# The first loads of a two-block transformer kernel in quarters and halves, with 11 warm-up matmuls in place of 16

## Chip, cores and metric

One core of one Trainium2 chip. The metric is device time of one execution in microseconds (us), lower is better.

## What is computed

Two blocks in sequence on a stream of 256 tokens with 1,024 features, all in float32. The part that the change touches is the very first projection of the first block, in which index queries for sparse attention are made from the input:

```python
q, k, v, g, qi, wi, ki = jnp.split(x @ w_in, cuts, axis=-1)
q = apply_rope(q.reshape(b, s, N_HEADS, HEAD_DIM), cos, sin)
...
qi = apply_rope(qi.reshape(b, s, IDX_HEADS, IDX_DIM), cos, sin)
ki = apply_rope(ki[:, :, None, :], cos, sin)[:, :, 0, :]
```

Some 150 such weight chunks follow: the rest of the attention, a second mixer, memory cross-attention, convolution and feed-forward layers.

## The kernel before

All weights are streamed from HBM in chunks of 1 MB (128 partitions x 2 halves x 1,024 columns) through four slots of `raw`. SP issues every load of the stream (lines 419 to 456). The first four chunks are issued at once, between them the input (`x_half`, line 425, into `h`, the residual stream, 8 tiles of 128 features), the indexer's small weights (`kiw`, kept in `v`), the constants `cs` and the vectors `vec`. Every later chunk waits until its slot has been split.

A product in float32 is done as three passes of a rounded format. ScalarE copies a half chunk into `wh`, which rounds it (`hi`, line 1079, copy at 1090). VectorE subtracts that from `raw` and keeps the rest in `wl` (`lo`, line 1592, at 1598). The input is split in the same way into `xh` and `xl`, two tiles at a time (`x_high`, line 1141; `x_low`, which executes at line 1668). TensorE multiplies high by high, high by low and low by high.

TensorE starts with `WARM_UP` matmuls on ones (line 816), whose results are not used. Then `project_tokens` (line 574) does the index queries, chunk by chunk: a half chunk has 12 products of 512 columns (2 token tiles x 2 feature tiles x 3 passes, line 594). For chunks 0 and 1 it goes in the order high x high, high x low of the input, low x high of the weights, so that the roundings can arrive late; chunk 0 needs four input tiles, two for each half, and chunk 1 the other four. Among the products of chunk 1 stand 16 small key products (`indexer_keys`, line 821, two passes each), eight behind each half. Chunks 2 to 5 are the queries (`qa`). Their code has the evacuations and rotations of earlier chunks woven in by tables of hooks and calls:

```python
hi(0)
act.wait_ge(x_in[0], 16)
x_high(0, None)
x_high(1, None)
hi(1)
...
chunks("qi", units(0))
chunks("qa", units(2), between={(1, 0): keep_indexer, (1, 1): memory_in, (2, 0): lambda: relu(0),
```

The order on each engine is the order of the program. ScalarE, after the rounding of half-chunk 6 (the first half of chunk 3), copies the two finished index-query banks out of PSUM (`rope_raw`, line 1125), then rounds half-chunk 7. VectorE makes the rest of half-chunk 7 and then rotates the first copy (`rotate`, line 1632, executing at lines 1626 and 1646). TensorE turns the rotated heads with four transposes (`turn_unit`, line 826, at 834); the first turn is hooked in after the first token tile of chunk 2's second half, the second after that of chunk 3's first half. Roundings beyond the first two chunks also wait for `w_used`, which counts the half chunks that TensorE has finished with.

Of the kernel before, what the change touches and what calls it, by code (L numbers as in the profile page):

```python
# [60 lines left out]
NCST = _at  # L61


WARM_UP = 16


class Phase:
# [132 lines left out]
def build(nc, w, xt, memt, vecs, cst, wkw, dft, rpb, gain, out):  # L200
    ctx = ExitStack()
    with ctx:
# [3 lines left out]
        def sem(name):  # L206
            return ctx.enter_context(nc.semaphore(name))
# [154 lines left out]


        raw_full = [sem(f"raw_full{i}") for i in range(RAW_SLOTS)]
        first_half = sem("first_half")
        x_in = [sem(f"x_in{i}") for i in range(2)]
        const_in, kiw_in = sem("const_in"), sem("kiw_in")
        mem_in, m_saved, m_back = sem("mem_in"), sem("m_saved"), sem("m_back")
        k_saved, k_back = sem("k_saved"), sem("k_back")
# [50 lines left out]
        def _(sp):  # L420
# [1 line left out]
                sp.dma_start(raw[:, slot, :, :], w[n]).then_inc(raw_full[slot], 16)  # L422


            def x_half(i):
                sp.dma_start(h[:, 4 * i:4 * i + 4, :], xt[:, 4 * i:4 * i + 4, :]).then_inc(x_in[i], 16)

            sp.dma_start(raw[:, 0, 0, :], w[0][:, 0, :]).then_inc(first_half, 16)
            x_half(0)
            sp.dma_start(raw[:, 0, 1, :], w[0][:, 1, :]).then_inc(raw_full[0], 16)  # L430
            x_half(1)
            load(1, 1)
            sp.dma_start(kiw, wkw).then_inc(kiw_in, 16)
            load(2, 2)
            sp.dma_start(cs[:, :], cst).then_inc(const_in, 16)
# [24 lines left out]
        def _(pe):  # L460
# [113 lines left out]
            def project_tokens(name, oh, ol, ready=None, hooks={}, tile0=0, order=(0, 1, 2)):  # L574
# [4 lines left out]
                for c in range(p.n):  # L579
                    n = p.n0 + c  # L580
                    slot = n % 2
                    for half in range(2):
                        early = ready is not None and c < 2
                        if early:

                            hi_, lo_ = ready(4 * c + 2 * half)
                            pe.wait_ge(*hi_)
                            pe.wait_ge(hi_ready, 2 * n + half + 1)
                        else:
                            pe.wait_ge(lo_ready, 2 * n + half + 1)  # L590

# [12 lines left out]
                            if c >= 2 and c % 2 == 0 and half == 0:  # L604
                                pe.wait_ge(evac[p.reader], p.base + c - 1 + t)

                        if early:
                            for q in order:
                                if q == 1:
                                    pe.wait_ge(lo_ready, 2 * n + half + 1)  # L610
                                if q == 2:
                                    pe.wait_ge(*lo_)
                                for t in range(2):
                                    for e in range(2):
                                        product(t, e, q, q == order[-1])
# [460 lines left out]
        def _(act):  # L1076
            chain = Chain(act, chain_act)

            def hi(h_):

                if h_ >= 2 * NCHUNK:
                    return
                n, j = divmod(h_, 2)
                if h_ == 0:
                    act.wait_ge(first_half, 16)
                elif j == 0 or h_ == 1:
                    act.wait_ge(raw_full[n % RAW_SLOTS], 16 * (n // RAW_SLOTS + 1))
                if h_ >= 4:
                    act.wait_ge(w_used, h_ - 3)
                act.activation(wh[:, n % 2, j, :], raw[:, n % RAW_SLOTS, j, :], ACT.Copy).then_inc(hi_ready, 1)  # L1090
# [140 lines left out]
            def units(u0):  # L1231
                return lambda c, t, b: rope_raw(u0 + 2 * c + t, t, b)

            hi(0)
            act.wait_ge(x_in[0], 16)
            x_high(0, None)
            x_high(1, None)
            hi(1)
            act.wait_ge(x_in[1], 16)
            x_high(2, None)  # L1240
            x_high(3, None)
            hi(2)
# [339 lines left out]
        def _(dve):  # L1582
# [9 lines left out]
            def lo(h_):  # L1592

                if h_ >= 2 * NCHUNK:
                    return
                n, j = divmod(h_, 2)
                dve.wait_ge(hi_ready, h_ + 1)
                dve.tensor_tensor(wl[:, n % 2, j, :], raw[:, n % RAW_SLOTS, j, :],  # L1598
                                  wh[:, n % 2, j, :].bitcast(F32), ALU.subtract).then_inc(lo_ready, 1)

# [165 lines left out]
            def plain_low(name, tiles, first):  # L1766
# [8 lines left out]
                                          ALU.subtract).then_inc(dve_evac, 1)  # L1775
                return f

            lo(0)
            x_low(0, "first", None)
            x_low(1, "first", None)  # L1780
            lo(1)
            x_low(2, "first", None)
# [594 lines left out]
```

## Time and profile before

| | |
|---|---|
| median of 3 runs | 991.11 us (990.96 to 991.43) |
| span of the profiled execution | 989.2 us |
| that span against the median | 1.9 us less |
| TensorE matmul busy | 972.1 us (98%) |
| VectorE, ScalarE, GpSimd busy | 69%, 56%, 21% |
| weights moved by SP's queue | 160.66 MB of 172.93 |
| mean granted TensorE clock | 0.998 |

The profile gives no total time of its own for the profiled execution, only its span from first to last instruction; times inside it count from the start of the span. A row names engine, line, tiles and duration; a bracket tells how long the engine stood idle before and what ended that. PEld is TensorE's weight load, which can run ahead of the matmul before it; SPq is SP issuing a transfer.

### The profile page before, as it was taken

How to read it: one execution, taken by the hardware profiler on the slowest of the kernel's cores; microseconds unless marked ns; L12 is line 12 of the kernel's file. 1: busy time of each engine (PE TensorE's matmuls, PEld its weight loads, DVE VectorE, ACT ScalarE, POOL GpSimd, SP SyncE). 2: the span in 40 equal slices, each digit the busy share in tenths (PEclk: the TensorE clock that was granted, in tenths of full speed). 3: DMA queues.
4: the chain of work that ended last, by engine and by line, in shares of the span. 5: the costliest groups of instructions: out<-in, count | busy, mean ns of one | idle time of the engine just before them, and what ended most of it. 6: DMA issues, size and time to landing. Idle time of an engine off the chain costs nothing.

```text
span 989.2 us, 16695 instructions
## 1 busy us (share of the span) xinstructions
PE 972.1 (98%) x6532; PEld 879.3 (89%) x6532; DVE 686.6 (69%) x1056; ACT 556.1 (56%) x856; POOL 209.3 (21%) x199
## 2 busy tenths in 40 slices
PE   9999989999999999999999999999999999999997
PEld 8779759989988988798899899999898989989985
DVE  5789785854666687665556779776687665767973
ACT  5556673665765474555355466555445555546662
POOL 0002034300344440012003005221044301202610
PEclk9999999999999999999999999999999999999999
DMA  9634425465334447246414655457546432555441
GB/s 363 241 132 166 175 87 208 162 221 214 128 128 141 174 133 271 108 171 213 150 64 170 213 186 187 181 194 281 186 170 255 163 135 93 198 183 181 172 152 43
DMA packets 24831, 172.93 MB, mean 175 GB/s; under 512 B 2752, under 2 KB 2880, under 8 KB 4416
## 3 DMA queue, kind: packets, MB, share of 16 engines
q1 hardware_dynamic: 23040, 160.66, 45.6%
q10 hardware_dynamic: 1728, 11.40, 3.0%
q8 instruction: 42, 0.69, 0.3%
q14 instruction: 21, 0.17, 0.1%
HBM read 166.81 MB, written 5.24 MB: 174 GB/s over the span
## 4 chain that ended last, share of the span: by engine, by line
PE 93%; DVE 2%; ACT 2%; DMA 1%; issue 1%; POOL 0%; SPq 0%; ACTq 0%; DVEq 0%
PE banks L506 38%; PE banks L594 16%; PE banks L512 14%; PE banks L514 7%; PE banks L504 6%; PE banks L656 4%; PE banks L710 1%; DMA raw<-w 1%; PE banks L761 1%; PE banks L762 1%; DVE work L1725 1%; PE banks L743 1%; PE banks L917 1%; PE banks L834 0%; DVE work L1737 0%
## 5 line engine op out<-in xcount | busy, mean ns | idle before, releaser
L1598 DVE TENSOR_TENSOR wl<-raw,wh 128x1024 fp32r<-128x1024 f32 x300 | 379.7, 1275 | 157.4 <-ACT wh L1090 156.0
L1090 ACT ACTIVATE wh<-raw 128x1024 fp32r<-128x1024 f32 x300 | 313.2, 1054 | 180.6 <-PE banks L506 76.1
L512 PE MATMUL banks<-xx,wh 128*128 128x512 f32 x544 | 192.5, 398 | 0.0
L506 PE MATMUL banks<-xx,wh 128*128 128x256 f32 x1024 | 190.3, 284 | 0.0
L506 PE MATMUL banks<-yy,wh 128*128 128x256 f32 x1024 | 187.8, 285 | 0.1
L506 PEld LDWEIGHTS banks<-xx,wh 128*128 128x128 f32 x1024 | 161.4, 192 | 1.4 <-issue 0.5
L506 PEld LDWEIGHTS banks<-yy,wh 128*128 128x128 f32 x1024 | 160.4, 192 | 0.7 <-issue 0.5
L514 PE MATMUL banks<-xx,wl 128*128 128x256 f32 x544 | 151.8, 279 | 0.0
L506 PE MATMUL banks<-xx,wl 128*128 128x256 f32 x512 | 144.8, 283 | 0.0
L506 PE MATMUL banks<-yy,wl 128*128 128x256 f32 x512 | 138.6, 283 | 0.0
L512 PEld LDWEIGHTS banks<-xx,wh 128*128 128x128 f32 x544 | 102.0, 187 | 22.7
L594 PE MATMUL banks<-wh,xx 128*128 128x512 f32 x352 | 113.2, 400 | 1.6 <-ACT kt L1258 0.7
L514 PEld LDWEIGHTS banks<-xx,wl 128*128 128x128 f32 x544 | 102.6, 189 | 0.3
L506 PEld LDWEIGHTS banks<-yy,wl 128*128 128x128 f32 x512 | 98.2, 192 | 0.2
L506 PEld LDWEIGHTS banks<-xx,wl 128*128 128x128 f32 x512 | 98.1, 192 | 0.1
L594 PEld LDWEIGHTS banks<-wh,xx 128*128 128x128 f32 x352 | 65.6, 188 | 18.0 <-issue 3.1
L594 PE MATMUL banks<-wl,xx 128*128 128x512 f32 x176 | 64.9, 391 | 0.0
L2185 POOL TENSOR_TENSOR work<-work,qz 128x512 f32<-128x512 f32 x18 | 29.2, 1624 | 134.3 <-ACT work L1513 133.0
L2148 POOL TENSOR_TENSOR acc<-work 128x256 f32<-128x256 f32 x9 | 9.2, 1027 | 201.0 <-ACT work L1139 201.0
L1147 ACT ACTIVATE xx<-h,vec 128x256 fp32r<-128x256 f32 x48 | 21.8, 502 | 43.9 <-DVE h L1709 32.7
L2151 POOL TENSOR_TENSOR acc<-acc,work 128x256 f32<-128x256 f32 x27 | 29.8, 1102 | 71.5 <-ACT work L1139 70.5
L1952 DVE TENSOR_TENSOR qz<-banks,qz 128x512 f32<-128x512 f32 x30 | 20.7, 690 | 29.4 <-ACT qz L1107 25.0
(221 smaller groups left out, 1449.3 us busy)
## 6 DMA issues: line engine op xcount, KB each, us to landing
raw<-w SPq DMA_DIRECT2D x149, 1024.0 KB, 4.8
m_scratch<-yy ACTq DMA_DIRECT2D x2, 1024.0 KB, 5.9
k_scratch<-kt ACTq DMA_DIRECT2D x2, 1024.0 KB, 8.2
kt<-k_scratch ACTq DMA_DIRECT2D x2, 1024.0 KB, 5.8
yy<-m_scratch ACTq DMA_DIRECT2D x2, 1024.0 KB, 6.0
raw<-w SPq DMA_DIRECT2D x2, 512.0 KB, 5.2
h<-xt SPq DMA_DIRECT2D x2, 512.0 KB, 6.1
v<-memt ACTq DMA_DIRECT2D x1, 1024.0 KB, 7.7
```

What stands on the lines that cost most here:

```text
L504: return pe.matmul(b[:, j, at], weights, o_[:, kk, :], start=k0 + k == 0 and q == 0, stop=k0 + k == KT * p.deep - 1 and q == 2, skip_group ...
L506: return pe.matmul(b[:, j, :], weights, o_[:, kk, :], start=k0 + k == 0 and q == 0 and (j == 0 or not both_open), stop=k0 + k == KT * p.de ...
L512: pe.matmul(b[:, j, :], wh[:, slot, j, k * P:k * P + P], operand[:, :, tile0 + k0 + k, :], start=k0 + k == 0, stop=False, skip_group_check ...
L514: return pe.matmul(b[:, j, 0:S], wl[:, slot, j, k * P:k * P + P], oh[:, tile0 + k0 + k, :], start=False, stop=k0 + k == KT * p.deep - 1, s ...
L594: mm = pe.matmul(bank[p.pair + t][:, :], (oh, oh, ol)[q][:, tile0 + k, t * P:t * P + P], (wh, wl, wh)[q][:, slot, half, e * 2 * CW:(e + 1) ...
L656: mm = pe.matmul(bank[(p.pair ^ 2 * block) + t][:, :], (yh, yh, yl)[q][:, k, t * P:t * P + P], (wh, wl, wh)[q][:, slot, half, e * 2 * CW:( ...
L1090: act.activation(wh[:, n % 2, j, :], raw[:, n % RAW_SLOTS, j, :], ACT.Copy).then_inc(hi_ready, 1)
L1147: ins = act.activation(xh[:, m, :], h[:, m, :], ACT.Copy, scale=vc(gain, m))
L1598: dve.tensor_tensor(wl[:, n % 2, j, :], raw[:, n % RAW_SLOTS, j, :], wh[:, n % 2, j, :].bitcast(F32), ALU.subtract).then_inc(lo_ready, 1)
L1952: chain(dve.tensor_tensor(d, b[0], d, ALU.add))
L2151: chain(pool.tensor_tensor(acc[:, :], acc[:, :], part[:, 0, :], ALU.add))
L2185: pool.tensor_tensor(wk3(7 + c % 2), a, b, ALU.mult).then_inc(pf_ready, 1)
```

## The change

The first half of chunk 0 and the first half of the input are each loaded in two quarters, in turn: weights, input, weights, input. The second half of the input stays one transfer. Chunk 1 is loaded in two halves, each with a semaphore of its own. The roundings, the rests and the products of the first half chunk follow by quarters. The warm-up is 11 matmuls.

```diff
-WARM_UP = 16
+WARM_UP = 11
...
-            sp.dma_start(raw[:, 0, 0, :], w[0][:, 0, :]).then_inc(first_half, 16)
-            x_half(0)
+            def x_tiles(i, a, b):
+                sp.dma_start(h[:, a:b, :], xt[:, a:b, :]).then_inc(x_in[i], 16)
+
+            Q = HALF // 2
+            sp.dma_start(raw[:, 0, 0, 0:Q], w[0][:, 0, 0:Q]).then_inc(first_quarter, 16)
+            x_tiles(0, 0, 2)
+            sp.dma_start(raw[:, 0, 0, Q:], w[0][:, 0, Q:]).then_inc(first_half, 16)
+            x_tiles(1, 2, 4)
             sp.dma_start(raw[:, 0, 1, :], w[0][:, 1, :]).then_inc(raw_full[0], 16)
-            x_half(1)
-            load(1, 1)
+            x_tiles(2, 4, 8)
+            sp.dma_start(raw[:, 1, 0, :], w[1][:, 0, :]).then_inc(second_half, 16)
+            sp.dma_start(raw[:, 1, 1, :], w[1][:, 1, :]).then_inc(raw_full[1], 16)
...
+                        if first:
+                            for e in range(2):
+                                pe.wait_ge(hi_ready if e else hi_first, 1)
+                                for t in range(2):
+                                    product(t, e, 0, False)
+                                if e == 0:
+                                    pe.wait_ge(*lo_)
+                                for t in range(2):
+                                    product(t, e, 2, False)
+                            for e in range(2):
+                                pe.wait_ge(lo_ready if e else lo_first, 1)
+                                for t in range(2):
+                                    product(t, e, 1, True)
...
-            hi(0)
+            act.wait_ge(first_quarter, 16)
+            act.activation(wh[:, 0, 0, 0:HALF // 2], raw[:, 0, 0, 0:HALF // 2], ACT.Copy).then_inc(hi_first, 1)
             act.wait_ge(x_in[0], 16)
             x_high(0, None)
+            hi(0)
+            act.wait_ge(x_in[1], 16)
             x_high(1, None)
             hi(1)
-            act.wait_ge(x_in[1], 16)
+            act.wait_ge(x_in[2], 16)
...
+            dve.wait_ge(hi_first, 1)
+            dve.tensor_tensor(wl[:, 0, 0, 0:HALF // 2], raw[:, 0, 0, 0:HALF // 2],
+                              wh[:, 0, 0, 0:HALF // 2].bitcast(F32), ALU.subtract).then_inc(lo_first, 1)
+            x_low(0, "first", None)
             lo(0)
-            x_low(0, "first", None)
```

SP's queue from the start of the program, before (`w` is the stream, `xt` the input):

```order
L428 DMA raw<-w 128x1024
L426 DMA h<-xt 128x1024
L430 DMA raw<-w 128x1024
L426 DMA h<-xt 128x1024
L422 DMA raw<-w 128x2048
L433 DMA v<-wkw 128x576
L422 DMA raw<-w 128x2048
L435 DMA cs<-cst 128x1664
L436 DMA vec<-vecs 128x240
L422 DMA raw<-w 128x2048
```

and after the change:

```order
L430 DMA raw<-w 128x512
L427 DMA h<-xt 128x512
L432 DMA raw<-w 128x512
L427 DMA h<-xt 128x512
L434 DMA raw<-w 128x1024
L427 DMA h<-xt 128x1024
L436 DMA raw<-w 128x1024
L437 DMA raw<-w 128x1024
L438 DMA v<-wkw 128x576
L423 DMA raw<-w 128x2048
L440 DMA cs<-cst 128x1664
L441 DMA vec<-vecs 128x240
```

Three transfers are added ahead of the indexer's weights; bytes and their order by chunk are the same, and chunk 3 still comes last.

ScalarE from its first rounding to the first half of chunk 3, before:

```order
L1090 ACTIVATE wh<-raw 128x1024 [waits first_half]
L1144 ACTIVATE xx<-h 128x512 [waits x_in0]
L1144 ACTIVATE xx<-h 128x512
L1090 ACTIVATE wh<-raw 128x1024 [waits raw_full0]
L1144 ACTIVATE xx<-h 128x512 [waits x_in1]
L1144 ACTIVATE xx<-h 128x512
L1090 ACTIVATE wh<-raw 128x1024 [waits raw_full1]
L1090 ACTIVATE wh<-raw 128x1024
L1090 ACTIVATE wh<-raw 128x1024 [waits w_used,raw_full2]
L1090 ACTIVATE wh<-raw 128x1024 [waits w_used]
L1090 ACTIVATE wh<-raw 128x1024 [waits w_used,raw_full3]
```

and after the change:

```order
L1259 ACTIVATE wh<-raw 128x512 [waits first_quarter]
L1168 ACTIVATE xx<-h 128x512 [waits x_in0]
L1106 ACTIVATE wh<-raw 128x512 [waits first_half]
L1168 ACTIVATE xx<-h 128x512 [waits x_in1]
L1114 ACTIVATE wh<-raw 128x1024 [waits raw_full0]
L1168 ACTIVATE xx<-h 128x512 [waits x_in2]
L1168 ACTIVATE xx<-h 128x512
L1114 ACTIVATE wh<-raw 128x1024 [waits second_half]
L1114 ACTIVATE wh<-raw 128x1024 [waits raw_full1]
L1114 ACTIVATE wh<-raw 128x1024 [waits w_used,raw_full2]
L1114 ACTIVATE wh<-raw 128x1024 [waits w_used]
L1114 ACTIVATE wh<-raw 128x1024 [waits w_used,raw_full3]
```

The first rounding is cut in two with an input rounding between, and the first half of chunk 1 waits for a transfer of its own; from chunk 2 on the row of ScalarE is as it was.

TensorE's first half chunk, before and then after:

```order
L594 MATMUL banks<-wh,xx 128x512 [waits hi_ready,x_hi]
L594 MATMUL banks<-wh,xx 128x512 x3
L594 MATMUL banks<-wh,xx 128x512 [waits x_lo]
L594 MATMUL banks<-wh,xx 128x512 x3
L594 MATMUL banks<-wl,xx 128x512 [waits lo_ready]
L594 MATMUL banks<-wl,xx 128x512 x3
```

```order
L601 MATMUL banks<-wh,xx 128x512 [waits hi_first,x_hi]
L601 MATMUL banks<-wh,xx 128x512
L601 MATMUL banks<-wh,xx 128x512 [waits x_lo]
L601 MATMUL banks<-wh,xx 128x512
L601 MATMUL banks<-wh,xx 128x512 [waits hi_ready]
L601 MATMUL banks<-wh,xx 128x512 x3
L601 MATMUL banks<-wl,xx 128x512 [waits lo_first]
L601 MATMUL banks<-wl,xx 128x512
L601 MATMUL banks<-wl,xx 128x512 [waits lo_ready]
L601 MATMUL banks<-wl,xx 128x512
```

The same 12 products, with four waits by quarter in place of three by half.

## Rows read from the trace of the kernel before

**Rows 1.** Page, parts 1 and 4: busy time, and the chain that ended last.

```profile
PE 972.1 (98%) x6532; PEld 879.3 (89%) x6532; DVE 686.6 (69%) x1056; ACT 556.1 (56%) x856; POOL 209.3 (21%) x199
...
PE 93%; DVE 2%; ACT 2%; DMA 1%; issue 1%; POOL 0%; SPq 0%; ACTq 0%; DVEq 0%
```

**Rows 2.** Timeline of SP, first 6 us: start, duration, issue.

```profile
0.75 0.39 SPq L428 DMA_DIRECT2D raw<-w  x1
...
3.38 0.50 SPq L433 DMA_DIRECT2D v<-wkw  x1
...
5.41 0.46 SPq L422 DMA_DIRECT2D raw<-w  x1
```

**Rows 3.** Timeline of ScalarE, 0 to 27 us.

```profile
4.78 1.06 ACT L1090 ACTIVATE wh<-raw 128x1024 fp32r<-128x1024 f32 x1 [2.75 <-DMA raw<-w]
6.02 1.15 ACT L1144 ACTIVATE xx<-h 128x512 fp32r<-128x512 f32 x2 [0.18 <-DMA h<-xt]
8.15 1.06 ACT L1090 ACTIVATE wh<-raw 128x1024 fp32r<-128x1024 f32 x1 [0.98 <-DMA raw<-w]
9.46 1.15 ACT L1144 ACTIVATE xx<-h 128x512 fp32r<-128x512 f32 x2 [0.25 <-DMA h<-xt]
11.93 2.01 ACT L1090 ACTIVATE wh<-raw 128x1024 fp32r<-128x1024 f32 x2 [1.31 <-DMA raw<-w]
...
20.04 1.06 ACT L1090 ACTIVATE wh<-raw 128x1024 fp32r<-128x1024 f32 x1 [2.89 <-DMA raw<-w]
21.01 1.07 ACT L1125 ACTIVATE work<-banks 128x512 f32<-128x512 f32 x2
21.96 1.06 ACT L1090 ACTIVATE wh<-raw 128x1024 fp32r<-128x1024 f32 x1
25.34 1.06 ACT L1090 ACTIVATE wh<-raw 128x1024 fp32r<-128x1024 f32 x1 [2.32 <-PE banks L594]
```

**Rows 4.** Timeline of TensorE's matmuls, 0 to 14 us (x32: two passes each).

```profile
1.00 5.67 PE L816 MATMUL banks<-ones 128*128 128x128 f32 x32 [1.00 <-POOL half L2141]
6.70 2.24 PE L594 MATMUL banks<-wh,xx 128*128 128x512 f32 x8
...
9.69 1.98 PE L594 MATMUL banks<-wh,xx 128*128 128x512 f32 x8
11.51 1.07 PE L594 MATMUL banks<-wl,xx 128*128 128x512 f32 x4
13.13 2.08 PE L594 MATMUL banks<-wh,xx 128*128 128x512 f32 x8 [0.56 <-ACT wh L1090]
```

**Rows 5.** Timeline of VectorE, 22.5 to 31 us.

```profile
23.05 1.23 DVE L1598 TENSOR_TENSOR wl<-raw,wh 128x1024 fp32r<-128x1024 f32 x1 [0.70 <-ACT wh L1090]
24.20 1.29 DVE L1626 TENSOR_TENSOR work<-work,cs 128x512 f32<-128x512 f32 x2
25.52 0.76 DVE L1646 TENSOR_TENSOR work<-work 128x256 f32<-128x256 f32 x2
26.43 1.23 DVE L1598 TENSOR_TENSOR wl<-raw,wh 128x1024 fp32r<-128x1024 f32 x1 [0.16 <-ACT wh L1090]
```

**Rows 6.** Timeline of TensorE's weight loads: the first two turns.

```profile
26.33 0.47 PEld L834 LDWEIGHTS banks<-cs,work 128*128 128x128 f32 x4 [0.15 <-DVE work L1646]
...
29.71 0.42 PEld L834 LDWEIGHTS banks<-cs,work 128*128 128x128 f32 x4 [0.33 <-DVE work L1646]
```

**Rows 7.** Two stretches: length, busy per engine (instructions), granted clock, DMA share, GB/s.

```profile
5.50:7.00 1.50, 1.47 (x12) 1.28 (x11) 1.13 (x1) 1.32 (x3) 0.00 (x0) 1.00 0.84 249
7.00:12.00 5.00, 5.00 (x23) 3.90 (x22) 3.73 (x6) 2.46 (x5) 0.00 (x0) 1.00 1.03 426
```

**Rows 8.** Timeline of TensorE: warm-up passes around 4.5 and around 5.4 us.

```profile
4.15 0.85 PE L816 MATMUL banks<-ones 128*128 128x128 f32 x3
...
5.06 0.61 PE L816 MATMUL banks<-ones 128*128 128x128 f32 x4
```

**Rows 9.** DMA issues of the first 10 us: KB each, us from issue to landing.

```profile
v<-wkw SPq DMA_DIRECT2D x1, 288.0 KB, 9.3
```

More of the change, by code:

```diff
@@ L364, in build @@
         raw_full = [sem(f"raw_full{i}") for i in range(RAW_SLOTS)]
-        first_half = sem("first_half")
-        x_in = [sem(f"x_in{i}") for i in range(2)]
+        first_quarter, first_half, second_half = sem("first_quarter"), sem("first_half"), sem("second_half")
+        hi_first, lo_first = sem("hi_first"), sem("lo_first")
+        x_in = [sem(f"x_in{i}") for i in range(3)]
         const_in, kiw_in = sem("const_in"), sem("kiw_in")
@@ L422, in load @@
                 sp.dma_start(raw[:, slot, :, :], w[n]).then_inc(raw_full[slot], 16)
-            def x_half(i):
-                sp.dma_start(h[:, 4 * i:4 * i + 4, :], xt[:, 4 * i:4 * i + 4, :]).then_inc(x_in[i], 16)
-            sp.dma_start(raw[:, 0, 0, :], w[0][:, 0, :]).then_inc(first_half, 16)
-            x_half(0)
+            def x_tiles(i, a, b):
[5 more added lines that the diff above has]
+            x_tiles(1, 2, 4)
             sp.dma_start(raw[:, 0, 1, :], w[0][:, 1, :]).then_inc(raw_full[0], 16)
-            x_half(1)
-            load(1, 1)
+            x_tiles(2, 4, 8)
+            sp.dma_start(raw[:, 1, 0, :], w[1][:, 0, :]).then_inc(second_half, 16)
+            sp.dma_start(raw[:, 1, 1, :], w[1][:, 1, :]).then_inc(raw_full[1], 16)
             sp.dma_start(kiw, wkw).then_inc(kiw_in, 16)
@@ L583, in project_tokens @@
                         early = ready is not None and c < 2
+                        first = n == half == 0
                         if early:
@@ L587, in project_tokens @@
                             pe.wait_ge(*hi_)
-                            pe.wait_ge(hi_ready, 2 * n + half + 1)
+                            if not first:
+                                pe.wait_ge(hi_ready, 2 * n + half + 1)
                         else:
@@ L605, in free @@
                                 pe.wait_ge(evac[p.reader], p.base + c - 1 + t)
-                        if early:
+                        if first:
[11 more added lines that the diff above has]
+                                    product(t, e, 1, True)
+                        elif early:
                             for q in order:
@@ L1085, in hi @@
                     act.wait_ge(first_half, 16)
-                elif j == 0 or h_ == 1:
+                    act.activation(wh[:, 0, 0, HALF // 2:], raw[:, 0, 0, HALF // 2:], ACT.Copy).then_inc(hi_ready, 1)
+                    return
+                elif h_ == 2:
+                    act.wait_ge(second_half, 16)
+                elif j == 0 or h_ in (1, 3):
                     act.wait_ge(raw_full[n % RAW_SLOTS], 16 * (n // RAW_SLOTS + 1))
@@ L1597, in lo @@
                 dve.wait_ge(hi_ready, h_ + 1)
+                if h_ == 0:
+                    dve.tensor_tensor(wl[:, 0, 0, HALF // 2:], raw[:, 0, 0, HALF // 2:],
+                                      wh[:, 0, 0, HALF // 2:].bitcast(F32), ALU.subtract).then_inc(lo_ready, 1)
+                    return
                 dve.tensor_tensor(wl[:, n % 2, j, :], raw[:, n % RAW_SLOTS, j, :],
```

## Prediction

> **What bounds the kernel now.** I read the page first: TensorE is busy for 972.1 of 989.2 us, and 93% of the chain that ended last runs through it [rows 1]. So an earlier start counts only if no later wait of TensorE takes it back. The change touches the first 12 us, so next come the timelines of that stretch: SP for when transfers are issued, ScalarE for when they land, TensorE for what it does meanwhile.
>
> All first transfers sit in SP's queue by 5.9 us [rows 2]. ScalarE works them off in order, and each start behind a DMA wait marks a landing [rows 3]: first half of chunk 0 at 4.78, first half of x at 6.02, second half of chunk 0 at 8.15, rest of x at 9.46, chunk 1 at 11.93, chunk 3 at 20.04. TensorE warms up from 1.00 to 6.67, starts the 24 products of chunk 0 at 6.70, has issued them by about 12.4, and starts chunk 1 at 13.13, just after its rounding (11.93 + 1.06 = 12.99) [rows 3, 4]. This wait of about 0.7 us is the only long one near the front; the page and the critical chain end it with the landing of chunk 1.
>
> The place that decides comes 13 us later and is easily missed. The first turn of rotated heads (line 834) lies inside chunk 2's products. TensorE's weight load for it stood idle 0.15 us at 26.33 until VectorE had ended the rotation [rows 6]; the matmul before it hid that wait, so it cost nothing. Follow it back. The rotation ends at 25.52 + 0.76 = 26.28 and sits directly behind the rounding rest of 23.05 [rows 5]; that one follows ScalarE's rounding of 21.96; ahead of this stand two copies from 21.01 and the rounding from 20.04, with no idle time between them; and that one waited 2.89 us for chunk 3 to land [rows 3]. So from 20.04 to 26.33 there is a second chain, **landing of chunk 3, ScalarE, VectorE, turn**, which TensorE's own progress does not move, and in the kernel before TensorE reaches its end at the same moment as that chain does. Slack: none, within 0.15 us.
>
> **The change, part by part.**
>
> *Warm-up, 16 to 11.* Each warm-up is two passes. The last ones ran at 0.61 us for four overlapped (about 0.11 us a pass), the ones at 4.15 took 0.85 us for three (about 0.21 us a pass) [rows 8], which I read as the change from the 1.2 to the 2.4 GHz level (the granted clock behind it is 1.00 [rows 7]). Five fewer take off 10 x 0.11 = 1.1 us: the warm-up ends near 5.6 instead of 6.67. Work ahead of that is the same, so I expect the level to rise at the same time, shortly before 5 us.
>
> *Quarters.* The first quarter of weights and of x need 256 KB each. Together they are as many bytes as landed at 4.78 before, so the first product can start after that landing and one rounding of x of about 0.6 us (half of the 1.15 us pair [rows 3]): near 5.5, not 6.70. ScalarE's roundings are the same columns in more instructions; the added fixed part lies in DMA waits. The second half of chunk 0 does not arrive sooner, as no byte ahead of it is gone: 8.15, rounded at 9.21, first product near 9.35. Its 12 products, at 0.2275 us each (eight from 9.69 to 11.51 [rows 4]), end their issue near 12.1. TensorE's time won in the first half is lost waiting here.
>
> *Chunk 1 in halves.* Its first half needs 512 KB behind x: 9.46 + (11.93 - 9.46)/2 = 10.7, rounded by 11.76, product at 11.9. TensorE is there at 12.1. So chunk 1 starts at about 12.1 instead of 13.13: **1.05 us gained at that point**.
>
> *Where it goes.* Chunk 1, chunk 2's first half and the key products run without a wait, so TensorE reaches the first turn 1.05 us sooner, near 25.3. There it waits for the second chain, which starts with chunk 3. The order ahead of chunk 3 holds the same bytes, and the queue is full, so the landing keeps its place. The gain is given back at the turn, all of it. What remains is small: ScalarE's rounding at 25.34 waited 2.32 us for TensorE [rows 3], and through it VectorE stood idle 0.16 us at 26.43 [rows 5]. That wait goes, and the second turn, where the weight load waited 0.33 us and the matmul issue lost some of it [rows 6], can come up to 0.15 us sooner. I take -0.1 us.
>
> *What the smaller pieces cost the stream.* SP issues three more transfers, at about 0.45 us each [rows 2]: chunk 3 is issued near 7 instead of 5.41, still 13 us ahead of its landing, so nothing. But one megabyte now moves in 2 KB rows instead of 4 KB ones, and chunk 1 in 4 KB rows. The trace has no 2 KB row. The nearest is the 288 KB of indexer weights in 2.3 KB rows: landed at 3.38 + 9.3 = 12.68 [rows 2, 9], 0.77 us behind chunk 1, or 383 GB/s, where chunk 1's megabyte took 2.47 us, 424 GB/s. At that rate a megabyte costs 2.74 us: +0.27 us on everything behind it. Lower bound: nothing or a gain, since the start of the stream is not at full rate anyway (from 5.5 to 7.0 us it moved 249 GB/s, after that 426 [rows 7], 0.6 us lost); upper bound +0.6 us, if the small rows meet as long a slow stretch again. I take +0.27, the price of the nearest row. Size alone did not slow a queued transfer: the first half of x took 6.02 - 4.78 = 1.24 us for 512 KB, 423 GB/s, as fast per byte as chunk 1. The Trainium skill ("DMA: Bandwidth & Descriptors", section Measured) says the opposite, that transfers should be batched to a megabyte or more; its table has 138 GB/s at 64 KB and 341 at 1 MB, so by it, as an estimate, the first megabyte in quarters would lose 0.6 us or more against the rows' 2.47. Its figures are for transfers issued by GpSimd; these rows, queued from SP, disagree.
>
> **Sum.** +1.05 us gained at chunk 1 and given back at the turn = 0; -0.1 behind the turn; +0.27 for chunk 3's later landing: +0.17 us. The profiled span of 989.2 us lies 1.9 us under the median of 991.11, which is time around the span that the change leaves alone. 991.11 + 0.17 = **991.3 us**, own range 990.8 to 991.9. That 16 warm-ups end later than the first landing, or that the first quarter may land hardly sooner than the half did because most of its time is not bytes, changes nothing here: the slack in front of the second half of chunk 0 takes it up (that half starts at 9.35; the first is through near 8.4, which is 5.5 plus 12 products and two short waits).
>
> **Rivals.**
>
> *The front gain stays.* If chunk 3 lands sooner too, the turn moves with it. For it: the slow stretch from 5.5 to 7.0 us falls on the second half of chunk 0 (8.15 - 6.02 = 2.13 us for 512 KB, against 1.24 for x); with another cut it may go, which is worth 0.6 us to all that follows. Against it: no byte is saved, and most of 20 us of landing time runs at 420 GB/s. Price: from -0.6 to the full -1.05 us, 990.1 us.
>
> *The halves of chunk 1 run slowly too.* The half of chunk 0 above took 0.89 us more than a half of x of the same size and shape. If that comes from reading half rows of the weights, chunk 1's two halves each pay it: +1.8 us on chunk 3, at the turn +1.6, 992.7 us. Against it: a slow stretch that belongs to the start of the program would look the same.
>
> *Slower: the clock does not rise in time.* With 11 warm-ups the steady stretch ends 1.1 us sooner, and then come gaps (x's rest, the second half's wait near 8.4 to 9.3). In the trace the level rose under steady passes from 1.00 on, and the next work came at once [rows 4, 8]. If it has not risen before the gaps, products cost nearly twice as much: 0.2275 x 0.21/0.11 = 0.43 us. All 24 would then take 24 x 0.2 = 4.8 us longer; warm-ups end near 6.2, chunk 0 near 16.5, chunk 1 starts 3.3 us later than now, and this side of the turn has no slack: 994.2 us. It decides from about five products at the low level on (1.05 us / 0.2); fewer are absorbed. Against it: nothing before 5 us changes, where the rise lay. The Trainium skill ("TensorE: Matmul & The Clock Gate", Part 1) says that the throttle is released by activity and that the moment varies from run to run; the pace in this trace agrees on the first, and one profile cannot show the second.
>
> **Chances.** Forecast 0.66, front gain stays 0.18, slow halves 0.10, clock 0.06. The range from 989.9 to 992.3 holds the first two with the spread of the runs (0.5 us) and part of the third. A measurement of this kernel tells about 0.2%, 2 us, from no change. Faster by more than that needs nearly twice the front gain: 0.04. Slower by more: the clock case and the worst of the slow halves: 0.08. Within: 0.88.
>
> **What would show it.** Right: warm-up over near 5.6, first product near 5.5, a gap before the second half's products near 9.3, chunk 1's products from about 12.1, and then **a new idle time of about 1 us of TensorE near 25.3 to 26.5, ahead of the first turn, ended by VectorE's rotation**, with ScalarE's rounding of chunk 3 still starting near 20.0 to 20.6. Wrong: no such wait, or chunk 3's rounding before 19.6 (the gain stays) or after 21 (slow halves); passes of 0.43 us in chunk 0 (the clock).

## The result and the profile after

| | before | change |
|---|---|---|
| median, measured together (9 runs each) | 991.19 us (990.96 to 991.49) | 993.41 us (992.51 to 994.56) |
| ratio | | 1.0024, 95% interval 1.0015 to 1.0032 |
| profiled execution: time, span | span 989.2 us | 992.51 us, span 990.7 us |
| mean granted TensorE clock of the profile | 0.998 | 0.998 |

The change is slower by 2.2 us, where 0.2 were forecast. The profiled execution is the fastest of its nine, 1.5 us longer in span than that of before; so the profile explains 1.5 of the 2.2 us, and the spread of the runs, 2 us wide where before it was half of one, is a question of its own.

ScalarE's timeline after the change. A line is start, duration, engine, source line, operation, tiles; the bracket gives the idle time before and what ended it.

```profile
4.12 0.63 ACT L1259 ACTIVATE wh<-raw 128x512 fp32r<-128x512 f32 x1 [2.08 <-DMA raw<-w]
...
7.96 0.64 ACT L1168 ACTIVATE xx<-h 128x512 fp32r<-128x512 f32 x1 [1.95 <-DMA h<-xt]
9.81 1.06 ACT L1114 ACTIVATE wh<-raw 128x1024 fp32r<-128x1024 f32 x1 [1.22 <-DMA raw<-w]
11.11 1.16 ACT L1168 ACTIVATE xx<-h 128x512 fp32r<-128x512 f32 x2 [0.24 <-DMA h<-xt]
12.40 1.07 ACT L1114 ACTIVATE wh<-raw 128x1024 fp32r<-128x1024 f32 x1
13.66 1.06 ACT L1114 ACTIVATE wh<-raw 128x1024 fp32r<-128x1024 f32 x1 [0.20 <-DMA raw<-w]
...
21.79 1.06 ACT L1114 ACTIVATE wh<-raw 128x1024 fp32r<-128x1024 f32 x1 [2.87 <-DMA raw<-w]
...
25.94 1.07 ACT L1114 ACTIVATE wh<-raw 128x1024 fp32r<-128x1024 f32 x1 [1.17 <-PE banks L601]
```

The first quarter of the weights is there at 4.12, but the second quarter of the input only at 7.96, and the second half of chunk 0 at 9.81, where before it landed at 8.15 [rows 3]: **1.66 us late**. From there on hardly anything more is lost: chunk 3 comes at 21.79 against 20.04, 1.75 us late.

TensorE's matmuls, same stretch and columns:

```profile
1.00 5.07 PE L836 MATMUL banks<-ones 128*128 128x128 f32 x22 [1.00 <-POOL half L2175]
5.72 2.45 PE L601 MATMUL banks<-wh,xx 128*128 128x512 f32 x8
8.01 1.08 PE L601 MATMUL banks<-wl,xx 128*128 128x512 f32 x4
11.01 2.08 PE L601 MATMUL banks<-wh,xx 128*128 128x512 f32 x8 [1.93 <-ACT wh L1114]
12.93 1.08 PE L601 MATMUL banks<-wl,xx 128*128 128x512 f32 x4
13.85 1.98 PE L601 MATMUL banks<-wh,xx 128*128 128x512 f32 x8
...
28.08 0.66 PE L854 MATMUL banks<-cs,work 128*128 128x128 f32 x4 [0.88 <-DVE work L1677]
```

The products start 0.98 us sooner (5.72 against 6.70 [rows 4]) and then stop for 1.93 us in front of the second half of chunk 0. Chunk 1 starts at 13.85, 0.72 us later than before (13.13). And at the first turn TensorE waits once more, 0.88 us, for VectorE's rotation. VectorE and the weight loads of the two turns, first VectorE:

```profile
25.94 1.28 DVE L1657 TENSOR_TENSOR work<-work,cs 128x512 f32<-128x512 f32 x2
27.26 0.76 DVE L1677 TENSOR_TENSOR work<-work 128x256 f32<-128x256 f32 x2
```

```profile
28.07 0.42 PEld L854 LDWEIGHTS banks<-cs,work 128*128 128x128 f32 x4 [1.30 <-DVE work L1677]
...
31.21 0.47 PEld L854 LDWEIGHTS banks<-cs,work 128*128 128x128 f32 x4 [0.15 <-DVE work L1677]
```

The first turn stands at 28.07 instead of 26.33 [rows 6], 1.74 us later, as much as chunk 3 is late. Up to the second turn 0.24 us come back (31.21 - 28.07 = 3.14, before 29.71 - 26.33 = 3.38), and 1.74 - 0.24 = 1.5 us is the difference of the spans.

Where the stream lost it: stretches of the change's core, with length, busy time of PE, PEld, DVE, ACT, POOL, granted clock, DMA share and, last, GB/s; then the same stretch of before.

```profile
2.00:8.50 6.50, 6.50 (x31) 6.01 (x30) 1.95 (x3) 2.45 (x5) 0.00 (x0) 1.00 0.83 261
...
8.50:16.00 7.50, 5.58 (x25) 4.31 (x24) 5.57 (x6) 4.43 (x6) 0.00 (x0) 1.00 1.02 422
```

```profile
2.00:8.50 6.50, 6.47 (x37) 5.81 (x36) 2.43 (x3) 2.59 (x5) 0.00 (x0) 1.00 0.92 325
```

From 2.0 to 8.5 us the change moves 261 GB/s against 325, that is 64 GB/s x 6.5 us = 0.42 MB less, or 1.0 us at the full rate of 422; from 8.5 on it runs as fast as before. The rest of the 1.66 us is not in this view, but in another record of the trace: each transfer raises its semaphore in 16 steps, read here as one for each of the 16 DMA engines, and a landing is the last of them. For the second half of chunk 0 the steps lie between 7.07 and 8.13 us in before, with a mean of 7.57, and between 7.36 and 9.79 in the change, with a mean of 8.54. So the mean is 0.97 us late, which fits the bytes, and the last step another 0.69: the engines have drifted apart. For chunk 3 they are still 2.47 us apart (19.29 to 21.76), in before 1.06 (18.96 to 20.02).

### The profile page after: what moved, and what is told of

It reads as the page before. It is cut to its first block, busy times and chain, and to the rows that moved or that the text cites. A ratio compares the mean times of both kernels' runs of the same rounds, so it can differ in the third digit from the quotient of the medians.

```text
span 990.7 us, 16680 instructions
## 1 busy us (share of the span) xinstructions
PE 971.3 (98%) x6522; PEld 878.3 (89%) x6522; DVE 687.2 (69%) x1057; ACT 556.8 (56%) x857; POOL 209.3 (21%) x199
## 4 chain that ended last, share of the span: by engine, by line
PE 92%; DVE 2%; ACT 2%; DMA 1%; issue 1%; SPq 1%; POOL 0%; ACTq 0%; DVEq 0%
PE banks L511 37%; PE banks L601 15%; PE banks L517 14%; PE banks L519 7%; PE banks L509 6%; PE banks L676 4%; DMA raw<-w 1%; PE banks L730 1%; PE banks L781 1%; PE banks L782 1%; PE banks L763 1%; DVE work L1756 1%; PE banks L937 1%; PE banks L854 0%; DVE work L1768 0%
```

## The experiments

Two theories stood after this reading. **Stream**: the 2 KB rows of the quarters hold up the first 8 us, and the rest follows from that. **Clock**: the shorter warm-up and the gap behind the quarters cost TensorE its level. The experiments first took the change apart. The landings (starts of ScalarE's roundings, one profile each) of the kernels that are compared most are these:

| kernel | 2nd half of chunk 0 | chunk 1, all of it | chunk 3 | median, us |
|---|---|---|---|---|
| before | 8.15 | 11.93 | 20.04 | 991.19 |
| weight_quarters | 8.51 | 12.25 | 20.36 | 991.51 |
| input_quarters | 8.83 | 12.58 | 20.68 | 991.62 |
| not_in_turn | 9.20 | 12.97 | 21.09 | 992.6 |
| quarters_only | 9.58 | 13.33 | 21.46 | 993.32 |
| the change | 9.81 | 13.66 | 21.79 | 993.41 |
| late_rows | 8.49 | 12.55 | 20.61 | 991.59 |
| halves_only | 8.21 | 12.05 | 21.47 | 992.29 |
| halves_order | 8.16 | 12.01 | 17.73 | 990.28 |
| warm11_only | 8.29 | 12.08 | 20.20 | 991.26 |
| before_order | 8.40 | 12.20 | 17.92 | 991.15 |

In the first six rows the distance from the second half of chunk 0 to chunk 3 is 11.85 to 11.98 us: whatever is lost is lost ahead of that half. How much a landing varies by itself shows where nothing ahead of it was changed: in before, halves_only, halves_order and its repetition, warm11_only and before_order the second half of chunk 0 comes between 8.15 and 8.40.

### The parts of the change

**warm16**: the change with the old warm-up.

```diff
-WARM_UP = 11
+WARM_UP = 16
```

> The change with 16 warm-up matmuls. Theory stream (the smaller first transfers delay the stream, and chunk 3's late landing sets the first turn): the same as the change, 993.4 us within 0.7, chunk 3's rounding again near 21.8 us and not 20.0. Theory clock (too short a warm-up leaves products slow): back at 991.2 us, with the spread of the runs as small as before (0.5 us).

Measured: 992.57 us (992.23 to 996.67), ratio 1.0019 (1.001 to 1.0029); second half of chunk 0 at 9.77, chunk 3 at 21.73, TensorE waiting 0.9 us in front of that half and 0.9 at the turn. Most of the loss stays without the short warm-up: 1.33 us above the kernel before as measured beside it (991.24), where the change lost 2.22. What makes up the other 0.9 us no run shows. **warm11_only** is the other side, the kernel before with 11.

```diff
-WARM_UP = 16
+WARM_UP = 11
```

> The kernel before with 11 warm-up matmuls and nothing else. Theory stream: 991.2 us within 0.3, chunk 3's rounding near 20.0 us. Theory clock: slower than before by 1 to 3 us, with a wide spread.

Measured: 991.26 us (991.19 to 991.73), ratio 1.0 (0.9991 to 1.001). Five warm-up matmuls fewer cost nothing by themselves; TensorE merely stands idle sooner.

**halves_only**: the kernel before with chunk 1 in two halves.

```diff
-            load(1, 1)
+            sp.dma_start(raw[:, 1, 0, :], w[1][:, 0, :]).then_inc(second_half, 16)
+            sp.dma_start(raw[:, 1, 1, :], w[1][:, 1, :]).then_inc(raw_full[1], 16)
```

> The kernel before with chunk 1 in two halves and nothing else (11 first issues, chunk 1 in 4 KB rows). Theory stream, if the half rows of the weights are what is slow: chunk 3's rounding 1 to 1.8 us later than 20.0 and the time 992 to 993 us. If the 2 KB rows of the quarters are: no change, 991.2 us within 0.3, chunk 3's rounding within 0.2 us of 20.0. Theory clock: 991.2 us.

Measured: 992.29 us (992.17 to 993.82), ratio 1.0014 (1.0005 to 1.0024): slower, and not for the reason that any theory had. ScalarE's timeline, then TensorE's first turn:

```profile
10.76 1.06 ACT L1093 ACTIVATE wh<-raw 128x1024 fp32r<-128x1024 f32 x1
12.05 1.06 ACT L1093 ACTIVATE wh<-raw 128x1024 fp32r<-128x1024 f32 x1 [0.23 <-DMA raw<-w]
15.28 2.00 ACT L1093 ACTIVATE wh<-raw 128x1024 fp32r<-128x1024 f32 x2 [2.16 <-DMA raw<-w]
21.47 1.06 ACT L1093 ACTIVATE wh<-raw 128x1024 fp32r<-128x1024 f32 x1 [4.18 <-DMA raw<-w]
```

```profile
27.76 0.66 PE L835 MATMUL banks<-cs,work 128*128 128x128 f32 x4 [1.89 <-DVE work L1649]
```

The halves land on time (12.05 against 11.93), and TensorE has no wait in front any more; it is 0.6 us ahead at the start of chunk 1 (12.52 against 13.13 [rows 4]) and 0.7 at the start of chunk 2 (21.49 against 22.23). Chunk 2 comes on time too. But chunk 3 comes 1.4 us late, and the turn makes TensorE wait 1.89 us. The queues of one half microsecond show a visitor, an instruction fetch (queue, kind: packets, MB, share of 16 engines); first halves_only from 18.5 to 19.0, then before from 19.5 to 20.0:

```profile
q1 hardware_dynamic: 25, 0.17, 83.0%
q8 instruction: 1, 0.02, 13.8%
```

```profile
q1 hardware_dynamic: 28, 0.22, 105.6%
q8 instruction: 1, 0.02, 13.7%
```

Over 1.5 us the fetch takes 4.6% of 16 engines, so 1.1 us of one engine. It starts at 18.83 here, at 19.65 in before, because TensorE has come to that instruction sooner: in all twelve profiles with 16 warm-ups it starts when TensorE has begun 191 to 195 of its recorded matmuls and weight loads, at 18.83 us here as at 30.47 in more_issues below. By the 16 steps of the semaphore, 15 shares of chunk 3 had landed by 20.15 and the last at 21.45. In before the same straggler sits on chunk 4: 15 shares by 22.50, the last at 23.79, and ScalarE rounds that chunk only from 25.34 on [rows 3]. The Trainium skill ("Runtime: NRT & Kernel Launch", Instruction fetch mechanics) says that a sequencer fetches its program in blocks of 16 KiB over a DMA queue of its own and that the cost is mostly hidden; size and queue agree with the 0.02 MB packet, and here it was not hidden. That the fetch lay on the engine of the last share is read from the times, as the trace doesn't name a packet's engine. No run moved the fetch alone, but halves_order below takes chunk 3 out of its way.

**quarters_only**: the change with chunk 1 in one transfer.

```diff
-            sp.dma_start(raw[:, 1, 0, :], w[1][:, 0, :]).then_inc(second_half, 16)
-            sp.dma_start(raw[:, 1, 1, :], w[1][:, 1, :]).then_inc(raw_full[1], 16)
+            load(1, 1)
```

> The change with chunk 1 in one transfer again (quarters and 11 warm-up matmuls stay, 12 first issues). Theory stream, if the quarters are what is slow: 993 us or more, chunk 3's rounding at 21.5 us or later. If the halves of chunk 1 are: 991.4 us within 0.4. Theory clock: 993.4 us as the change, but with chunk 3's rounding near 20 us.

Measured: 993.32 us (991.96 to 994.0), ratio 1.0019 (1.001 to 1.0029), with the landings of the change within 0.35 us. The quarters carry the loss. This profile shows something else as well: TensorE idle for 2.06 us, and then the low level.

```profile
10.78 3.65 PE L600 MATMUL banks<-wh,xx 128*128 128x512 f32 x8 [2.06 <-ACT wh L1111]
```

```profile
10.80:14.10 3.30, 3.30 (x8) 2.62 (x9) 2.30 (x3) 1.92 (x3) 0.00 (x0) 0.50 1.02 424
14.20:16.00 1.80, 1.80 (x9) 1.48 (x9) 1.58 (x2) 1.14 (x2) 0.00 (x0) 1.00 0.98 412
```

In these 3.3 us the granted clock is 0.50 (1.2 GHz), and eight products take 3.65 us instead of 2.08. The profile of the change had a gap of nearly the same length, 1.93 us, and kept 1.00.

**weight_quarters** and **input_quarters** take the quarters apart: of the weights alone (16 warm-ups, chunk 1 and input as before), and of the input alone.

```diff
-            sp.dma_start(raw[:, 0, 0, :], w[0][:, 0, :]).then_inc(first_half, 16)
-            x_half(0)
+            sp.dma_start(raw[:, 0, 0, 0:Q], w[0][:, 0, 0:Q]).then_inc(first_quarter, 16)
+            x_tiles(0, 0, 4)
+            sp.dma_start(raw[:, 0, 0, Q:], w[0][:, 0, Q:]).then_inc(first_half, 16)
```

> Only the weights' first half in quarters (11 first issues), the input in halves and chunk 1 whole as before, 16 warm-up matmuls. If the slowness goes by short rows or issues alike, this has half of it: chunk 3's rounding near 20.8 us, 991.9 us within 0.4. If it lies with the input's quarters: 20.1 us and 991.2 us. If with the weights': 21.5 us and 992.5 us.

```diff
-            x_half(0)
+            x_tiles(0, 0, 2)
+            x_tiles(1, 2, 4)
```

> The kernel before with the first half of the input in two quarter transfers, and nothing else. If the input's quarters are what holds the stream up: second half of chunk 0 rounded from 9.2 or later (8.15 before, 8.51 with the weights' quarters alone), chunk 3's rounding from 21.0 or later, median 992.0 to 993.0. If each pair of quarters costs the same small sum: second half of chunk 0 near 8.5, chunk 3 near 20.4, median 991.3 to 991.6. If only the two together cost (more than the sum of both): as in the second case, and chunk 3 in neither kernel alone explains the 1.75 us of the change.

Measured: weights 991.51 us (991.26 to 992.49), ratio 1.0 (0.9991 to 1.001); input 991.62 us (991.33 to 992.65), ratio 1.0005 (0.9996 to 1.0014). On chunk 3 the weights' quarters cost 0.32 us and the input's 0.64: together 0.96, where quarters_only lost 1.42. Neither is the culprit alone, and the weights' 0.32 is little more than a landing varies by itself.

**not_in_turn**: quarters_only with both quarters of the weights first, then both of the input.

```diff
-            x_tiles(0, 0, 2)
             sp.dma_start(raw[:, 0, 0, Q:], w[0][:, 0, Q:]).then_inc(first_half, 16)
+            x_tiles(0, 0, 2)
```

> quarters_only with both quarters of the weights issued ahead of both quarters of the input, not in turn; the same rows, bytes and waits. If the rows and transfers themselves cost: second half of chunk 0 from 9.4 to 9.8, chunk 3 from 21.2 to 21.7, 992 to 994 as quarters_only. If going back and forth between two tensors costs: second half of chunk 0 from 8.5 to 8.9, chunk 3 from 20.4 to 20.8, 991.4 to 991.8.

Measured: 992.6 us (991.13 to 994.15), ratio 1.0014 (1.0005 to 1.0024), between the two expectations: chunk 3 is 1.05 us late, about the 0.96 of the two parts. So going back and forth may cost the other 0.4 us; the second half of chunk 0 came at 9.58 to 10.11 in the profiles of all the six kernels with the quarters in turn, and at 9.20 here. Six of the ten runs lie above 992.5, four of them with a mean clock of 0.996 or 0.997. The mean of the 16 steps tells it otherwise than the last of them: by it chunk 3 is late by 0.35 us with the weights' quarters, 0.75 with the input's, 0.82 in quarters_only and 0.42 here, so that the two parts make more than the whole. How the loss divides is not shown.

### Rows, number of transfers, or crowding

**late_rows** puts the short rows where the stream runs at full rate: chunk 1 in two transfers of 512 columns of both halves.

```diff
-            load(1, 1)
+            Q = HALF // 2
+            sp.dma_start(raw[:, 1, :, 0:Q], w[1][:, :, 0:Q]).then_inc(second_half, 16)
+            sp.dma_start(raw[:, 1, :, Q:], w[1][:, :, Q:]).then_inc(raw_full[1], 16)
```

> The kernel before with chunk 1 in two transfers of 2 KB rows (the first 512 columns of both halves, then the others), so that the short rows move when the stream is at its full rate; the roundings of chunk 1 wait for both. If short rows cost the price that was taken for them wherever they move: chunk 1 rounded from 12.2, chunk 3 from 20.3, 991.3 to 991.5. If they cost there what they cost in the first 8 us: chunk 1 from 13.3, chunk 3 from 21.4, 992.4 to 993. If short rows cost nothing once the stream runs: 11.9, 20.0, 991.2, and the loss belongs to the start alone.

```profile
9.80 1.15 ACT L1148 ACTIVATE xx<-h 128x512 fp32r<-128x512 f32 x2 [0.25 <-DMA h<-xt]
12.55 2.01 ACT L1094 ACTIVATE wh<-raw 128x1024 fp32r<-128x1024 f32 x2 [1.60 <-DMA raw<-w]
```

Measured: 991.59 us (991.4 to 991.7), ratio 1.0004 (0.9994 to 1.0014). From the rest of the input to chunk 1 it takes 12.55 - 9.80 = 2.75 us, in before 11.93 - 9.46 = 2.47 [rows 3]: 0.28 us for a megabyte, the price that the prediction took. Another 0.34 us are lost ahead of it, although nothing there was changed (second half of chunk 0 at 8.49). That is 0.09 us beyond 8.40, too little in one profile to say that the short rows behind it in the queue are felt. At full rate a megabyte in 2 KB rows costs a fifth of what one costs as quarters at the start.

**short_rows** has 2 KB rows and the old number of transfers: chunk 0 and both input transfers by column quarters, 512 KB each; the first products therefore wait for two transfers of each.

```diff
-            sp.dma_start(raw[:, 0, 0, :], w[0][:, 0, :]).then_inc(first_half, 16)
-            x_half(0)
-            sp.dma_start(raw[:, 0, 1, :], w[0][:, 1, :]).then_inc(raw_full[0], 16)
-            x_half(1)
+            Q = HALF // 2
+            hv, xv = [a.rearrange("p (a b) s -> p a (b s)", b=2) for a in (h[:, :, :], xt)]
+            sp.dma_start(raw[:, 0, :, 0:Q], w[0][:, :, 0:Q]).then_inc(first_half, 16)
+            sp.dma_start(hv[:, 0:4:2, :], xv[:, 0:4:2, :]).then_inc(x_in[0], 16)
+            sp.dma_start(raw[:, 0, :, Q:], w[0][:, :, Q:]).then_inc(raw_full[0], 16)
+            sp.dma_start(hv[:, 1:4:2, :], xv[:, 1:4:2, :]).then_inc(x_in[1], 16)
```

> The kernel before with as many first issues (10), each as large as before, but chunk 0 and the input in rows of 2 KB (each transfer takes two pieces of 2 KB of every partition). Theory rows: chunk 3's rounding at 21.3 us or later, 992.3 us or more. Theory issues (transfers smaller or more in number are what is slow): chunk 3's rounding near 20.2 us, 991.4 us within 0.4.

Measured: 997.68 us (996.96 to 998.17, 4 runs), ratio 1.0064. Chunk 3 landed at about 21.3, 1.3 us late, without one transfer more and with transfers of the old size. So 2 KB rows by themselves cost nearly what quarters_only lost (1.42). But two megabytes have them here and one there, so that the run doesn't show the rows to be all of it. The time says nothing: ScalarE loaded its table only behind the first wait (9.43 instead of 0.75), and TensorE had nothing to do until 12.35.

**more_issues** was to be the counterpart, long rows and more transfers: half chunk, half input and chunk 1 each in two transfers of 64 partitions.

```diff
+            for p in (slice(0, 64), slice(64, P)):
+                sp.dma_start(raw[p, 0, 0, :], w[0][p, 0, :]).then_inc(first_half, 16)
...
```

> The kernel before with 13 first issues but rows as long as before: first half of chunk 0, first half of the input and chunk 1 each in two transfers of 64 partitions. Theory rows: chunk 3's rounding within 0.3 us of 20.0, 991.2 us within 0.3. Theory issues (each further transfer costs the stream 0.5 us or so): chunk 3's rounding at 21.3 us or later, 992.5 us or more.

Measured: 1000.33 us (999.74 to 1001.82, 4 runs), ratio 1.009; first half of the input at 10.58 instead of 6.02, chunk 3 at 29.03. Transfers of 64 partitions are so much slower by themselves that the run doesn't tell rows from number.

**after_held**: the change, with SP holding back the indexer's weights and all that follows until the input's second quarter has landed.

```diff
+            sp.wait_ge(x_in[1], 16)
             sp.dma_start(kiw, wkw).then_inc(kiw_in, 16)
```

> The change, with SP waiting for the second quarter of the input before it issues the indexer's weights and all behind them, so that 8 transfers instead of 13 are in the queue at first. Theory crowding (the number of transfers queued behind is what slows the first ones): the input's second quarter lands near 6.0 us instead of 7.94, chunk 3 is rounded near 20.3 us, 991.6 us within 0.5. Theory rows (2 KB rows are what is slow): landings as in the change, 7.9 and 21.8 us, 993.4 us within 0.7.

Measured: 993.16 us (992.16 to 993.84), ratio 1.0019 (1.0009 to 1.0028); second half of chunk 0 at 9.85, chunk 3 at 21.80, as in the change. So the transfers from the indexer's weights on don't crowd out the first ones. After a gap of 2.24 us the clock fell here too, to 0.50 from 10.8 to 14.1 us.

```profile
11.05 3.52 PE L602 MATMUL banks<-wh,xx 128*128 128x512 f32 x8 [2.24 <-ACT wh L1115]
```

**gap_filled**: the change with eight unused matmuls on ones between the halves of chunk 0, which are added work.

```diff
+                            for _ in range(8):
+                                pe.matmul(bank[7][:, 0:P], ones[:, :], ones[:, :], start=True, stop=True)
```

> The change with 11 warm-up matmuls, and 8 more matmuls on ones between the halves of chunk 0, where TensorE stood idle for 1.9 us. Theory clock (with only 11 warm-ups the idle time between the halves of chunk 0 lets the granted clock fall in a part of the runs): median 992.6 us within 0.3 and a spread under 1 us, mean granted clock 0.997 or more in every run. Rival (the spread comes from the landings): as the change, 993.4 us median and 2 us of spread.

Measured: 993.41 us (992.5 to 994.24), ratio 1.002 (1.001 to 1.003). Mean clocks are now 0.997 to 0.999 in every run; the median has not moved, and the spread hardly (1.7 us against 2.1). So the clock is not the main cause; it adds to some runs of the versions with a gap, as change_order16 shows below.

### The second chain

**halves_order**: halves_only, with chunk 3 issued ahead of the constants and vectors, which are not needed before the rotation.

```diff
             load(2, 2)
+            load(3, 3)
             sp.dma_start(cs[:, :], cst).then_inc(const_in, 16)
             sp.dma_start(vec[:, :], vecs).then_inc(const_in, 16)
-            load(3, 3)
```

> The halves alone, and chunk 3 issued ahead of the constants and vectors (952 KB), 16 warm-up matmuls. Theory second chain (the front gain of about 1 us is real, and chunk 3's late landing takes it back at the first turn): chunk 3 rounded near 17.6 us and no wait of TensorE at the first turn; 990.2 us within 0.3, that is 2 us under the halves alone and 1 us under the kernel before. Rival (the halves cost time elsewhere): 992.3 us as the halves alone.

```profile
17.73 1.06 ACT L1093 ACTIVATE wh<-raw 128x1024 fp32r<-128x1024 f32 x1 [0.49 <-DMA raw<-w]
```

```profile
6.85 2.24 PE L595 MATMUL banks<-wh,xx 128*128 128x512 f32 x8 [0.63 <-ACT xx L1147]
```

Measured: 990.28 us (990.0 to 990.66) against 991.14, ratio 0.9991 (0.9981 to 1.0). The wait of 0.63 us ahead of 6.85 is TensorE's only one up to the first turn. The gain of the halves comes through as soon as chunk 3 is out of the way. **halves_order_again** is the same kernel, measured once more on another chip.

> The kernel of halves_order once more, unchanged, for its interval: 990.3, 0.9 us faster than the kernel before (ratio 0.9991, interval below 1). If its first measurement was luck of the landings: 990.8 to 991.4.

Measured: 990.31 us (990.01 to 990.82) against 991.25, ratio 0.9991 (0.9982 to 1.0). The interval touches 1, but all 21 runs of the two lie below all 46 runs of before beside them (the lowest of these is 990.87). It is the only version faster than both kernels, by 0.9 us.

**before_order** has the new order alone.

> The kernel before, chunk 3 issued ahead of the constants and vectors. Theory second chain: there is no wait of TensorE there to win but 0.1 us, so 991.1 us within 0.2. Rival (the order of the loads is itself worth 1 us or more): 990.2 us or less.

Measured: 991.15 us (990.99 to 991.31), ratio 0.9999 (0.999 to 1.0009). An earlier chunk 3 is worth nothing while TensorE isn't ahead. **change_order16** gives the change the same order and 16 warm-ups.

> The change with chunk 3 issued ahead of the constants and vectors and 16 warm-up matmuls. Theory second chain: no wait at the first turn; what is left of the loss is the late second half of chunk 0 (9.8 us against 8.15), which starts chunk 1's products near 13.8 us instead of 13.13: 991.8 us within 0.4. Rival (the quarters cost something behind the first 30 us): 992.5 us as with 16 warm-ups alone.

Measured: 992.29 us (991.28 to 994.52), ratio 1.0015 (1.0006 to 1.0025). No wait is left at the turn; in the profile (991.91) TensorE waits 2.21 us for the second half of chunk 0, and that remains.

```profile
11.14 2.08 PE L601 MATMUL banks<-wh,xx 128*128 128x512 f32 x8 [2.21 <-ACT wh L1114]
```

Six runs lie from 991.28 to 992.48 at a mean clock of 0.998, four from 993.65 to 994.52 at 0.996.

## Why the prediction was wrong

*What bounds the kernel*: right. The second chain, from the landing of chunk 3 to the first turn, took 6.28 us (21.79 to 28.07), before 6.29. The turn moved as chunk 3 moved. before_order shows that an early chunk 3 is worth nothing without TensorE's lead, and halves_order that the two together gain 0.9 us. The lead alone, with chunk 3 at its old place, was not run, as in halves_only chunk 3 came 1.4 us late.

*Warm-up*: near in its time, but not for the reason given. By its row it ended at 6.07 where 5.6 was forecast, and the first product started beside its last passes at 5.72, where 5.5 was forecast. The level, which was to rise shortly before 5 us as before, had not risen by then:

```profile
5.00 0.85 PE L836 MATMUL banks<-ones 128*128 128x128 f32 x3
```

Three passes in 0.85 us is the slow pace of the row at 4.15 [rows 8], where before had four in 0.61 from 5.06 on. The trace's record of a granted clock of 1.00 begins at 6.49 in the change and at 4.88 in before. warm11_only shows no cost of the short warm-up by itself.

*Quarters*: **the step that failed**. "The second half of chunk 0 does not arrive sooner, as no byte ahead of it is gone: 8.15." It didn't arrive sooner, but 1.66 us later. I argued from bytes; what changed was their cut (256 KB a transfer, rows of 2 KB, weights and input in turn), in the one stretch where the stream isn't at its rate; short_rows points to the rows. With that, chunk 1 started at 13.85 instead of the forecast 12.1, and the gain of 1.05 us at that point became a loss of 0.72. TensorE's wait at the turn, 0.88 us, looks like the wait of about 1 us that was forecast, but for another reason: TensorE was late, and chunk 3 was later still.

*The price of the rows*: the same failure in the sum. +0.27 us for the megabyte in 2 KB rows was right for the full rate, from which its row came (0.28 in late_rows), and wrong by a factor of five for the start (1.42 in quarters_only, of which the mean of the 16 steps is 0.82 and the drift of the engines the rest). By the rows that it names, the distance behind chunk 1 is 12.68 - 11.93 = 0.75 us and not 0.77, which makes 393 GB/s and +0.20; nothing hangs on that. The upper bound, +0.6, had the right thought, a slow stretch met by small rows, but took the length of the old slow stretch as the limit. That the trace had no 2 KB row at the start was a reason for a wider range. For the 0.7 us between the profile's 1.5 and the median's 2.2, and for runs up to 994.56, two things are at hand: landings that vary (in the six profiles with quarters in turn the second half of chunk 0 spans 9.58 to 10.11) and, in some runs, the low clock after the gap. Their shares were not separated.

The Trainium skill's rule ("DMA: Bandwidth & Descriptors", section Measured), which was set aside there, pointed the right way: batch transfers to a megabyte or more, and an estimate of 0.6 us or more lost. Size alone is not it, though: chunk 1 in two transfers of 512 KB with 4 KB rows landed 0.12 us off its old place, and in late_rows two of 512 KB with 2 KB rows cost 0.28 us. What no figure of its table shows is that the start costs several times that.

*Chunk 1 in halves*: right relative to the stream. Its first half came 12.40 - 9.81 = 2.59 us behind the second half of chunk 0, where 10.7 - 8.15 = 2.55 was forecast. The gain of 1.05 us measured 0.86 and 0.94 in the medians of halves_order and its repetition. By TensorE's rows the lead was smaller, 0.57 us at chunk 1 (12.56 against 13.13) and 0.69 at the first turn (25.75 against 26.44).

*Behind the turn*: right in sign; 0.24 us came back, where 0.1 was taken. ScalarE's wait for TensorE fell from 2.32 to 1.17 us.

*The rivals*: "the halves of chunk 1 run slowly" gave 992.7, near the result, with the wrong culprit: the halves landed in time, the quarters ahead of them didn't. "The clock does not rise in time" (994.4 by its own sum, not 994.2) occurred in part: in the profile the clock rose at 6.49, when two products had started, where it was to decide from about five on; from then on it was 1.00. The views show 1.00 ahead of 6.49 too, where the trace has no record. What occurs besides in some runs is a fall after a gap. "The front gain stays" needs chunk 3 earlier, and comes true in halves_order.

What remains open: why the finer cut costs so much in the first 8.5 us and lets the engines drift apart, how much of it is due to the rows and how much to the size, number and order of the transfers, and whether the alternation, of which one profile with ten runs tells, really costs 0.4 us. Open too is why the medians with the quarters in turn and 11 warm-ups (993.16 to 993.41) lie above that of warm16 (992.57).

## What to carry to other kernels

A stretch in which a resource is not at its rate has its own prices: take the cost of a transfer from the stretch in which it will run, not from one at full rate. When an earlier start is argued, follow the next wait behind it back to its own source, and move that too; here moving one line, which alone is worth nothing, turned a loss of 1.1 us into a gain of 0.9. And cutting a first transfer finer brings the first piece sooner but may delay all the rest.

## What the runs showed of the hardware

- An instruction fetch of 16 KB rides the DMA engines of the weights; it took one of them for 1.1 us. A lead of TensorE of 0.7 us made it start 0.82 us sooner, and the straggler, 1.3 us behind the other 15 shares, moved from chunk 4, which was not waited for, to chunk 3, which was.
- Two transfers of 64 partitions were far slower than one of 128 (more_issues): the same 512 KB of input landed at 10.58 instead of 6.02 us.
- TensorE's granted clock fell to 0.50 after idle gaps of 2.06 and 2.24 us in two profiles and stayed at 1.00 after one of 1.93 in the change and one of 2.21 in change_order16. The Trainium skill ("TensorE: Matmul & The Clock Gate", Part 1) says that idle time brings the throttle back and that the moment of its release varies between runs. Both agree: the first record of 1.00 begins at 3.92 us in halves_order and at 6.62 in its repetition, which is the same kernel.
- From 2.0 to 8.5 us the queues moved 325 GB/s in before and 261 in the change, against 422 to 424 afterwards, though issued transfers had not landed all that time. In the change the 16 steps of a landing lay 2.43 us apart at the second half of chunk 0 and 2.47 at chunk 3, in before 1.06 at both.
